# A hybrid decoder layer on one core: eleven steps of the mixing stage moved in a hand-written order

## The reference

```python
def layer(x, c, ...):
    mod = jax.nn.silu(c) @ w_ada + b_ada            # shift, scale and gate of both halves
    h = rmsnorm(x, norm1_g) * (1.0 + sc1) + sh1
    proj = h @ w_in                                  # xr, gr, q, k, v, o, ig, fg, u
    y_a = rglru(causal_dwconv(xr)) * gelu(gr)        # 384 wide
    hm, C1, n1, m1 = mlstm(q, k, v, ig, fg, ...)     # 4 heads of 96, chunks of 128 tokens
    y_b = sigmoid(o) * rmsnorm(hm, mlstm_norm_g)
    y_c = pool_mix(u, pool_buf, ...)                 # windows of 2, 4, 8, 16; 256 wide
    x = x + gt1 * (concatenate([y_a, y_b, y_c]) @ w_out)
    h2 = rmsnorm(x, norm2_g) * (1.0 + sc2) + sh2
    return x + gt2 * (square(relu(h2 @ w_ff1)) @ w_ff2)

# mlstm, one chunk: carry C, n, m
S   = (q @ k.T) * exp(D - m_t)
num = S @ v + inter * (C @ q);  den = sum(S) + inter * (n @ q)
h   = num / maximum(abs(den), exp(-m_t))
C   = decay * C + sum(w * v * k)
```

## Time and profile before

| what | value |
|---|---|
| median of 3 runs | 1176.22 us |
| the profiled execution's own time | 1175.78 us |
| its span | 1174.0 us |
| TensorE matmuls busy | 1124.6 us (96%) |
| VectorE busy | 792.8 us (68%) |
| ScalarE busy | 473.4 us (40%) |
| GpSimd busy | 346.9 us (30%) |

### The profile page before, as it was taken

One profiled execution on the slowest core, in us unless ns is written; L12 is line 12 of the kernel. 1 busy time (PEld: TensorE's weight loads), 2 busy tenths in 40 slices (PEclk: granted clock), 3 DMA queues, 4 the chain that ended last, 5 costly groups with the idle time before them and its releaser, 6 DMA issues.

```text
span 1174.0 us, 19681 instructions
## 1 busy us (share of the span) xinstructions
PE 1124.6 (96%) x7237; PEld 1077.3 (92%) x7237; DVE 792.8 (68%) x1319; ACT 473.4 (40%) x780; POOL 346.9 (30%) x275
## 2 busy tenths in 40 slices
PE   4799999999989999999999999999999999999997
PEld 1598888888979999899999999999999999999996
DVE  4561455478775434678578878778778788788546
ACT  5551355655456344642233332332432433433431
POOL 0442011201434357764032022132131231231352
PEclk9699999998989999999999999999999999999998
DMA  8912523566523722111111111202102202111104
GB/s 302 326 57 88 142 90 126 177 180 218 176 87 113 269 90 73 54 55 37 37 36 55 54 37 55 71 18 71 56 16 75 68 18 72 53 50 58 37 1 145
DMA packets 67846, 109.85 MB, mean 94 GB/s; under 512 B 6435, under 2 KB 42567, under 8 KB 67399
## 3 DMA queue, kind: packets, MB, share of 16 engines
q1 hardware_dynamic: 57574, 84.88, 22.0%
q10 hardware_dynamic: 10208, 24.12, 6.6%
HBM read 96.81 MB, written 12.18 MB: 93 GB/s over the span
## 4 chain that ended last, share of the span: by engine, by line
PE 82%; DVE 9%; ACT 3%; DMA 2%; issue 1%; POOL 1%; SPq 1%; ACTq 0%; POOLq 0%; DVEq 0%
PE D L2407 7%; PE D L2409 7%; PE D L2408 7%; PE D L2591 6%; PE D L2593 5%; PE D L2592 5%; PE X L2593 5%; PE X L2591 5%; PE X L2592 5%; PE X L2663 5%; PE X L2664 5%; PE X L2665 5%; PE D L2663 2%; PE D L2665 2%; PE D L2664 2%; DMA RAWW<-in_WADA 2%
## 5 line engine op out<-in xcount | busy, mean ns | idle before, releaser
L2407 PE MATMUL D<-H_hi,W_hi 128*128 128x344 f32 x472 | 158.6, 336 | 3.7 <-POOL H_lo L1087 3.1
L2409 PE MATMUL D<-H_hi,W_lo 128*128 128x344 f32 x472 | 152.4, 323 | 0.0
L2408 PE MATMUL D<-H_lo,W_hi 128*128 128x344 f32 x472 | 152.4, 323 | 0.0
L1087 POOL TENSOR_TENSOR Y_lo<-FU,Y_hi 128x344 fp32r<-128x344 f32 (+3 forms) x84 | 100.1, 1194 | 154.2 <-ACT Y_hi L1521 88.5
L1082 POOL TENSOR_TENSOR W_lo<-RAWW,W_hi 128x1024 fp32r<-128x1024 f32 x25 | 61.6, 2465 | 182.5 <-ACT W_hi L1234 182.2
L1087 POOL TENSOR_TENSOR Y_lo<-EY,Y_hi 128x344 fp32r<-128x344 f32 (+1 forms) x24 | 38.3, 1598 | 216.3 <-ACT Y_hi L1521 144.5
L2407 PEld LDWEIGHTS D<-H_hi,W_hi 128*128 128x128 f32 x472 | 90.5, 192 | 11.8 <-issue 7.6
L2408 PEld LDWEIGHTS D<-H_lo,W_hi 128*128 128x128 f32 x472 | 90.3, 191 | 0.9 <-issue 0.5
L2409 PEld LDWEIGHTS D<-H_hi,W_lo 128*128 128x128 f32 x472 | 90.2, 191 | 0.0
L2215 DVE SCALAR_TENSOR_TENSOR X<-X,MOD 128x344 f32<-128x344 f32 (+1 forms) x138 | 75.7, 566 | 9.2 <-PE X L2665 9.0
L2663 PE MATMUL X<-Y_hi,W_hi 128*128 128x344 f32 x252 | 80.7, 320 | 0.0
(11 more groups left out here) (416 smaller groups left out, 3455.1 us busy)
## 6 DMA issues: line engine op xcount, KB each, us to landing
RAWW<-in_W SPq DMA_DIRECT2D x76, 512.0 KB, 3.6
RAWW<-in_WADA ACTq DMA_DIRECT2D x28, 512.0 KB, 4.1
RAWW<-in_WADA SPq DMA_DIRECT2D x20, 512.0 KB, 8.0
RAWW<-in_W ACTq DMA_DIRECT2D x18, 512.0 KB, 3.7
X0T<-in_x SPq DMA_DIRECT2D x3, 1376.0 KB, 12.8
out_y<-OUTN SPq DMA_DIRECT2D x24, 172.0 KB
X<-in_x SPq DMA_DIRECT2D x8, 344.0 KB, 5.3
NM<-nm_d SPq DMA_DIRECT2D x8, 256.0 KB, 5.3
```

Source lines behind the costliest of these rows:

```text
L1087: nc.gpsimd.tensor_tensor(lo_v, fu_v, hi_v.bitcast(F32), ALU.subtract).then_inc(lo_ready, 1)
L2407: T.matmul(out, w_h, hi[:, kt, a:b], start=(kt == 0), stop=False)
L2408: T.matmul(out, w_h, lo[:, kt, a:b], start=False, stop=False)
L2409: one = T.matmul(out, w_l, hi[:, kt, a:b], start=False, stop=(kt == KT - 1))
```

## The change

Words of the table are moved; none is added or removed, and no other line of the kernel is changed. In the recurrence, `AB:0` goes behind `D:9:2`, `S:1 SX:1 SMB:0` behind `D:10:0`, `SMB:1` behind `HN:2` and `SMB:2` behind `SX:3`. In the last third, `YD:0` goes ahead of `HN:4`, `W:15` behind `HN:5`, `ADM:21` directly behind `ADT:21`, `NU:6` directly behind `AB:6`, the first two pool products ahead of `D:14:2`, `ADT:22 ADM:22 HN:6 LD:7 HM:6` behind `D:15:0`, and `W:17` from `D:16:1` to `D:15:2`.

```diff
-D:9:1 R:46 R:45 LD:1 ADM:16 EX:0 ADA:17:0 S:0 SX:0 ADA:17:1 W:11 AB:0 R:47
-D:9:2 ADT:17 U:0 NU:0 HN:0 CN:0 ADM:17 HM:0 EX:1 ADA:18:0 SMK S:1 SX:1 SMB:0
-D:10:0 LD:2
+D:9:1 R:46 R:45 LD:1 ADM:16 EX:0 ADA:17:0 S:0 SX:0 ADA:17:1 W:11 R:47
+D:9:2 AB:0 ADT:17 U:0 NU:0 HN:0 CN:0 ADM:17 HM:0 EX:1 ADA:18:0 SMK
+D:10:0 S:1 SX:1 SMB:0 LD:2
 D:10:1 LD:3 AB:1 NU:1 ADA:18:1 U:1 CN:1 HN:1
 D:10:2 HM:1 R:49 R:48 LD:4 EX:2 W:12
-D:11:0 SMB:1 S:2 SX:2 AB:2 NU:2 ADT:18 U:2 CN:2 ADM:18 HN:2 R:50
-D:11:1 SMB:2 HM:2 R:52 EX:3 ADA:19:0 S:3 SX:3
+D:11:0 S:2 SX:2 AB:2 NU:2 ADT:18 U:2 CN:2 ADM:18 HN:2 SMB:1 R:50
+D:11:1 HM:2 R:52 EX:3 ADA:19:0 S:3 SX:3 SMB:2
...
-D:12:2 R:56 U:4 ADT:20 HN:4 W:14 YD:0 R:58 HM:4 LD:6
+D:12:2 R:56 U:4 ADT:20 YD:0 HN:4 W:14 R:58 HM:4 LD:6
...
-D:13:1 S:5 ADA:21:1 POOLV:0 YS POOLS:0 POOLD:0 SX:5 W:15 YSD AB:5 NU:5 HN:5 HM:5
-D:13:2 ADT:21 R:59 U:5 CN:5
-D:14:0 Y:2 ADM:21 EX:6 YD:2
-D:14:1 ADA:22:0 S:6 SX:6 R:61 AB:6 ADA:22:1 Y:3 POOLV:1
-D:14:2 POOL:0:0 POOLS:1 NU:6 YD:3 R:60 POOLY:0:0 POOL:0:1 ADT:22 POOLY:0:1 HN:6 LD:7 POOL:0:2 POOLD:1 POOLY:0:2 ADM:22
-    HM:6
-D:15:0 U:6 Y:4 POOL:1:0 R:62 CN:6 POOLY:1:0 ADA:23:0 EX:7 POOL:1:1 W:16 R:64 YD:4
+D:13:1 S:5 ADA:21:1 POOLV:0 YS POOLS:0 POOLD:0 SX:5 YSD AB:5 NU:5 HN:5 W:15
+D:13:2 ADT:21 ADM:21 HM:5 R:59 U:5 CN:5
+D:14:0 Y:2 EX:6 YD:2
+D:14:1 ADA:22:0 S:6 SX:6 R:61 AB:6 NU:6 ADA:22:1 Y:3 POOL:0:0 POOLY:0:0 POOL:0:1 POOLY:0:1 POOLV:1
+D:14:2 POOL:0:2 POOLS:1 POOLY:0:2 YD:3 R:60 POOLD:1
+D:15:0 ADT:22 ADM:22 HN:6 LD:7 U:6 HM:6 POOL:1:0 Y:4 R:62 CN:6 POOLY:1:0 ADA:23:0 EX:7 POOL:1:1 W:16 R:64 YD:4
 D:15:1 POOLY:1:1 S:7 SX:7 POOL:1:2 POOLY:1:2 ADA:23:1 R:63
-D:15:2 Y:5 YD:5 AB:7 NU:7 ADT:23 HN:7
+D:15:2 W:17 Y:5 YD:5 AB:7 NU:7 ADT:23 HN:7
 D:16:0 R:65 HM:7 Y:6 U:7 YD:6 CN:7 ADM:23
-D:16:1 Y:7 W:17 YD:7
+D:16:1 Y:7 YD:7
 D:16:2
```

## The result

| | before | after |
|---|---|---|
| median of the runs, us | 1175.89 (1174.27 to 1178.18, 4 runs) | 1184.02 (1181.90 to 1185.84, 4 runs) |
| profiled execution: own time, span, us | 1175.78, 1174.0 | 1182.41, 1180.6 |

What follows compares the result with a forecast made beforehand. TensorE was busy for 96% of the span, so only its waits and clock could give time. Terms 0.7 + 1.7 + 3.0 + 1.5 = 6.9 us, less 0.7, gave 6.2 us and 1170.0 us; range 1165.5 to 1175.0.

Steps and rivals of the forecast that it cites:

- the allowance: Whole sum: 0.7 us taken off the 6.9 us gain for waits of tenths at a dozen bank changes.
- `AB:0`, `S:1`: Start of the recurrence: both waits, 1.00 and 0.92 us, fall under a dense unit each, 1.9 us gained.
- `SMB:1` behind `HN:2`: Value product of chunk 2: 0.5 us of wait left, no low clock after it, 3.3 us more gained.
- It can't keep it: At `AB:4`, chunk 4: TensorE waits 3 us, a new low-clock stretch costs 2.2 us, 0.7 us of lead left.
- rival 2: VectorE keeps up: wait at `AB:4` under 1.46 us, port clashes may fall elsewhere; 1166 to 1168 us, chance 0.22.
- `YD:0`, `ADM:21`: `ADT:20` and `Y:2`, ahead of `AB:6`: waits of 0.9 and 1.46 us removed, together 1.7 us gained.
- `NU:6` and the pool, `W:17`: Pool to first output matmul: 3.72 us wait and 2.8 us clock go, 3.0 us lead left at `Y:7`; `W:17` gives 1.5.
- rival 4: `POOLV:1` to `YD:6`: VectorE's list decides the stage's end, 2.1 us slower, 1178.3 us; chance 0.08.
- Rival 3: At `Y:7`: a 1.6 to 1.8 us wait for `YD:6` brings low clock, gain only 2 to 3, 1173.7 us; chance 0.22.

Runs made afterwards that it cites:

- early: Kernel before with only `AB:0` moved behind `D:9:2` and `S:1 SX:1 SMB:0` behind `D:10:0`; 1172.59 us, ratio 0.9975.
- r60: Changed kernel with `R:60`, the start of the load for `ADA:23:0`, moved directly behind `R:61`; 1182.02 us, ratio 1.0077 against the kernel before.
- smb12: Kernel before with only `SMB:1` moved behind `HN:2` and `SMB:2` behind `SX:3`; 1178.21 us, ratio 1.0017.
- rec: Kernel before with the four recurrence moves alone (`AB:0`, `S:1 SX:1 SMB:0`, `SMB:1`, `SMB:2`); 1176.76 us, ratio 1.0019.
- vlight: r60 with two of the four window sums of `POOLV:1` left out; 1179.71 us, ratio 1.0037 against the kernel before.
- three: Kernel before with only the first three moves of the last third (`YD:0`, `W:15`, `ADM:21`); 1177.66 us, ratio 1.0023.

## Why the prediction was wrong

By the marks: start to A:2 is 2.6 us shorter, A:2 to A:4 3.7 longer (33.66 for 29.93), A:4 to A:6 3.3 longer and A:6 to out 2.4 longer, together +6.9. Summed, the steps had said -6.9 (-6.2 with the allowance). One reading was incomplete: the clock row is below 9 in a third slice, the last one, outside the stage of the change.

*`AB:0`, `S:1`.* Both waits went, as predicted. I walked no queue here, and `ADA:18:0` took 1.15 us back, 1.8 in early. The load of its weights stands on ScalarE's list behind another one, whose buffer `ADA:17:0` has to free first; both are issued from 231.12 us on, behind the start of `ADA:17:0`, and it can come no sooner than that.

*`SMB:1` behind `HN:2`.* Right up to A:2: no wait (0.5 us predicted), clock at 1.00, TensorE 2.6 us earlier there and 5.8 us at the end of the old low stretch (6.3 predicted).

*"It can't keep it."* The mechanism was right and the size wrong; this is the first mis-sized term. I gave 3 us of wait and 2.2 us of clock, 0.7 us of lead left. My own times gave 3.4 us (ready at 294.8, there at 291.4), and with those the 0.7 us came about. The wait was 3.41 us, and the low stretch 11 us long at 0.53: 5.2 us, more than twice my figure. Part of that is the luck of the execution, for by the same sum the same wait was followed by 5.1 us of low clock in r60 and smb12, 3.4 in rec and 1.7 in vlight. A:4 came 1.1 us later than before instead of 0.7 earlier, with 1.9 us of the low stretch's 5.2 still behind it. The place was wrong too: I watched `EX` and its value product, and the first thing TensorE needs is X3, for the transpose. VectorE's rows:

```profile
261.92 0.56 DVE L1891 TENSOR_TENSOR KW<-X,COL 128x384 f32<-128x384 f32 x1 [1.57 <-PE X L2497]
...
280.58 2.83 DVE L1988 SCALAR_TENSOR_TENSOR CS<-CS,S,TC 128x576 f32<-128x576 f32 x1
...
285.02 0.56 DVE L1899 TENSOR_TENSOR T<-X,COL 128x388 f32<-128x388 f32 x1
...
290.99 0.18 DVE L1716 TENSOR_TENSOR MOD<-X,COLS 128x18 f32<-128x18 f32 x1
...
314.37 1.60 DVE L1952 SCALAR_TENSOR_TENSOR ST<-UM,COLS,ST 64x8 f32<-64x8 f32 x1
...
335.97 0.52 DVE L1869 TENSOR_TENSOR FU<-GT,HS 128x344 f32<-128x344 f32 x1 [2.36 <-ACT GT L1330]
336.52 0.56 DVE L1891 TENSOR_TENSOR KW<-X,COL 128x384 f32<-128x384 f32 x1
337.11 0.69 DVE L1894 TENSOR_TENSOR EX<-X,EX 128x512 f32<-128x512 f32 x1
```

`MOD` ends 60.8 us after the start mark, 61.5 before: VectorE was 0.7 us ahead, not 2.0. From the start mark to this `MOD` it is busy for 49.0 us and idle for 11.8, where before has 49.3 and 12.2; so it was not full, and the idle time that I took away came back elsewhere. Ahead of chunk 2 the quarter had filled the time up to `KW`. Now VectorE waits there for TensorE, 1.57 us and then 0.36 and 0.58 (before, 0.97 and 0.99 behind `KW`). Its two quarters now stand together ahead of `NU:3` (285.02), where `CS` took 2.83 us for 0.82, beside the split of unit 13. That clash is not new. Before, the same split met `HM`:

```profile
286.86 2.62 DVE L1912 TENSOR_TENSOR HM<-NUM,SM 128x384 f32<-128x384 f32 x1
```

So the clash moved to another instruction and stayed as long, which is what rival 2 had hoped it would not do.

*`YD:0`, `ADM:21`.* Wrong: -1.7 predicted, and A:4 to A:6 grew by 3.3 us. Both old waits went, and `YS` waits 1.25 and `AB:6` 1.64 us instead, 0.4 us more idle time in all. The rest is the clock, 3.5 us: the tail of the stretch behind `S:4` and a new one behind `YS`. In three, the same moves alone, the waits are 1.66 and 1.64 us, and A:4 to A:6 is 37.7 us for 37.3. So the moves gained nothing and cost 0.4 us themselves; the low clock did the rest. Once `D:14:0` is done, the chain to `AB:6` runs over ScalarE and VectorE alone: from the gelu of that step to the end of `EX` it takes 8.5 us (329.31 to 337.80), 8.7 before (326.33 to 335.01), and `FU` ahead of `KW` waits the same 2.36 us for the next gelu. I had costed the chain at 0.8 us of gain; it gained 0.2.

*`NU:6` and the pool, `W:17`.* Wrong by the most: -4.5 predicted, +2.4 came. I forgot `R:60`. It is a transfer that ScalarE's queue issues in the table's order, behind `Y_hi` of `YD:3`, and `YD:3` stands behind the window sums in both kernels. With `NU:6` ahead of them, the window sums start 2.5 us behind the value product of chunk 6 (340.34 and 337.86 us) and not together with it (335.05 and 335.07 before), and their clash with `Y_lo` took 1.3 us, near the 1.0 that I gave. Counted from that product, `YD:3` comes 2.8 us and the transfer 3.9 us later than before. ScalarE and GpSimd after the change:

```profile
352.48 0.37 ACTq L555 DMA_DIRECT2D RAWW<-in_WADA  x1
```

```profile
279.82 2.97 POOL L1081 TENSOR_TENSOR W_lo<-RAWW,W_hi 128x1024 fp32r<-128x1024 f32 x1 [14.04 <-ACT W_hi L1233]
...
314.05 1.89 POOL L1059 TENSOR_TENSOR PA<-ST 128x1023 f32<-128x1023 f32 x1
...
374.36 2.40 POOL L1081 TENSOR_TENSOR W_lo<-RAWW,W_hi 128x1024 fp32r<-128x1024 f32 x1
```

The transfer was issued at 345.81 us in the kernel before, and `ADA:23:0` now waits 3.74 us for it. The load is only the first thing that was late: with it cured, the lead is lost at `S:7` and the time stays (r60). For `W:17` I costed the wait it removes and not what its split runs beside: `Y:7` pays 1.70 us.

*Rivals.* The true course is rival 4's sign with a spread-out cause, of which rival 4 had one piece, `POOLV:1` to `YD:6`; I gave it 0.08. Its price rested on one place, while TensorE waited at six: `ADA:18`, `S:4`, `YS`, `AB:6`, `ADA:23` and `Y:7`. Rival 3's bar, a low clock from a wait of 1.67 us on, doesn't hold: the clock fell behind 1.25 and 1.64 us here and not behind the 1.70 us of `Y:7`. Of the port, the trace agrees with the page I cited, the Trainium skill, SBUF - State Buffer, section Who interferes with whom: each VectorE row above that grew (`CS`, `HM`, `ST`, `SM`) has two inputs in SBUF and runs beside a GpSimd instruction that reads SBUF.

## What to carry to other kernels

Removing a wait gains nothing if the engine that was waited for comes no sooner at the next place where it is needed: the wait comes back there. So before moving a step, follow the second engine's list, its own waits included, to that place. Here one wait of 3.4 us with its low clock cost more than a short one of 0.9 us earlier on, which left the clock up. Where a bank or buffer is shared by many steps, walk its whole chain of owners and every transfer issued on the moved step's queue; the wait goes to the next owner. And try the moves of a bundle apart: the eleven together cost 9 us, and two of them alone gain 2.9 (1.3 to 4.6).

## What the runs showed of the hardware

- The price of the low clock isn't fixed by the wait ahead of it: 3.41 us of wait brought 11 us at 0.53, while 3.74 us (at 358.64) brought 6 us at 0.72. Nor is it fixed for one place: behind the same 3.42 us at `S:4` it was 5.1 us in smb12, 3.4 in rec and 1.7 in vlight.
- Instructions of 4 to 18 elements took 0.9 to 1.6 us instead of 0.2 beside a GpSimd instruction that reads SBUF, and one of 128x576 2.83 us instead of 0.82.
- A transfer of 512 KB of weights on ScalarE's queue took 8.5 to 9.4 us from issue to landing around 230 us (medians of two, six kernels), and with its issue that sets how early `ADA:18` can run.
